# A three-block model on one core: products of constants on TensorE under the norms and turns, the head statistic of the gated linear attention in all partitions, the attention's modulation pair loaded beside its keys, the result stored in two halves

## What is computed

```python
x   = first_block(...)          # gated recurrence and gMLP in parallel, then a swiglu feed-forward, rmsnorm
mod = silu(c) @ mod_w[l] + mod_b[l]                       # 6 vectors for each layer l = 0, 1
h   = rmsnorm(x) * g * (1 + sc1) + sh1                    # "norm" below
y   = gla_mixer(h)         # layer 0: per head o = rmsnorm(o) over its 256 columns, times silu(og), @ w_out
y   = swa_sink_attention(h, w_q, sinks, w_out, k, v)      # layer 1: 16 heads, window of 128 keys
x   = x + g1 * y
h   = rmsnorm(x) * g' * (1 + sc2) + sh2
x   = x + g2 * peer(h)     # 16384 experts: hidden = gelu(h @ u.T), weighted by routes, @ v
k, v = shared_kv(rmsnorm(x) ...)                          # after layer 0
return rmsnorm(x) * g_final                               # 256 x 1024
```

## Time and profile before

| | |
|---|---|
| median of 3 runs | 2563.48 us (2561.51 to 2564.61) |
| the profiled execution's own time | 2558.92 us |
| its span, first to last instruction | 2557.1 us |
| busy: TensorE, VectorE, ScalarE, GpSimd | 97%, 71%, 49%, 3% of the span |
| mean granted TensorE clock | 0.984 of full speed |
| chain of waits that ended last | TensorE 86%, VectorE 6%, ScalarE 1%, DMA 1% |
| moved by DMA | 471.69 MB, 184 GB/s over the span |

### The profile page before, as it was taken

One profiled execution on the slowest core, in us unless ns is written; L12 is line 12 of the kernel. 1 busy time (PEld: TensorE's weight loads), 2 busy tenths in 40 slices (PEclk: granted clock), 3 DMA queues, 4 the chain that ended last, 5 costly groups with the idle time before them and its releaser, 6 DMA issues.

```text
span 2557.1 us, 43191 instructions
## 1 busy us (share of the span) xinstructions
PE 2470.6 (97%) x15988; PEld 2229.0 (87%) x15988; DVE 1808.5 (71%) x3476; ACT 1262.4 (49%) x2457; POOL 79.2 (3%) x42
## 2 busy tenths in 40 slices
PE   7999999999999999999999998889999999999997
PEld 4489889988899999999888887789999999888886
DVE  5566569863279967786888874759977787755554
ACT  2344134442234567775555453434557776445454
POOL 0000000000140000000000000041000000000000
PEclk9999999999999999999999999999999999999998
DMA  6553557645325543435888863143554344755552
GB/s 267 194 182 135 181 199 279 247 167 198 113 103 179 178 174 133 149 133 193 291 289 287 288 244 137 66 182 132 177 187 140 141 140 148 253 188 193 196 195 100
DMA packets 79176, 471.69 MB, mean 184 GB/s; under 512 B 8833, under 2 KB 9089, under 8 KB 26161
## 3 DMA queue, kind: packets, MB, share of 16 engines
q1 hardware_dynamic: 78480, 467.85, 51.4%
q10 hardware_dynamic: 272, 1.05, 0.1%
q0 software_dynamic: 272, 0.69, 0.1%
HBM read 468.51 MB, written 1.05 MB: 184 GB/s over the span
## 4 chain that ended last, share of the span: by engine, by line
PE 86%; DVE 6%; ACT 1%; DMA 1%; issue 1%; DVEq 0%; SPq 0%; ACTq 0%
PE bank L757 27%; PE bank L682 27%; PE bank L538 5%; PE bank L918 5%; PE bank L694 4%; PE bank L709 3%; PE bank L825 3%; PE bank L949 2%; PE bank L1013 1%; PE bank L548 1%; PE bank L1058 1%; PE bank L522 1%; DVE t_split L2002 1%; DVE macc L1744 1%; PE bank L554 1%
## 5 line engine op out<-in xcount | busy, mean ns | idle before, releaser
L682 PE MATMUL bank<-h_split,t_split 128*128 128x256 f32 x6144 | 772.3, 285 | 5.2 <-DVE t_split L2002 4.5
L682 PEld LDWEIGHTS bank<-h_split,t_split 128*128 128x128 f32 x6144 | 745.6, 192 | 7.5 <-DVE t_split L2002 5.9
L2002 DVE TENSOR_TENSOR t_split<-ring,t_split 128x1024 fp32r<-128x1024 f32 x512 | 624.9, 1221 | 159.5 <-ACT t_split L1236 158.0
L757 PE MATMUL bank<-t_split,w_split 128*128 128x512 f32 x3072 | 697.8, 390 | 1.1 <-ACT w_split L1243 1.1
L757 PEld LDWEIGHTS bank<-t_split,w_split 128*128 128x128 f32 x3072 | 576.5, 188 | 120.9 <-ACT w_split L1243 1.5
L1241 ACT ACTIVATE t_split<-ring 128x1024 fp32r<-128x1024 f32 x256 | 271.9, 1062 | 347.7 <-PE bank L757 219.4
L1236 ACT ACTIVATE t_split<-ring 128x1024 fp32r<-128x1024 f32 x256 | 271.0, 1059 | 295.1 <-PE bank L682 269.7
L2034 DVE TENSOR_TENSOR w_split<-arena,w_split 128x256 fp32r<-128x256 f32 x256 | 108.8, 425 | 194.0 <-ACT w_split L1243 193.6
L1163 ACT ACTIVATE arena<-bank 128x256 f32<-128x256 f32 (+2 forms) x160 | 63.8, 404 | 301.3 <-PE bank L709 68.1
L918 PE MATMUL bank<-h_split,wd_split 128*128 128x256 f32 x1056 | 129.2, 286 | 4.0 <-ACT h_split L1495 4.0
L918 PEld LDWEIGHTS bank<-h_split,wd_split 128*128 128x128 f32 x1056 | 128.1, 192 | 5.3 <-issue 4.3
(11 more groups left out here) (320 smaller groups left out, 2866.9 us busy)
## 6 DMA issues: line engine op xcount, KB each, us to landing
ring<-in_peer_u SPq DMA_DIRECT2D x128, 1024.0 KB, 4.9
ring<-in_peer_v SPq DMA_DIRECT2D x128, 1024.0 KB, 4.9
ring<-in_w_mod SPq DMA_DIRECT2D x24, 1024.0 KB, 5.0
ring<-in_mod_w SPq DMA_DIRECT2D x24, 1024.0 KB, 5.0
H<-in_mod_w SPq DMA_DIRECT2D x96, 256.0 KB, 5.2
ring<-in_w_in SPq DMA_DIRECT2D x22, 1024.0 KB, 5.7
ring<-in_w_up SPq DMA_DIRECT2D x22, 1024.0 KB, 4.9
ring<-in_peer_wq SPq DMA_DIRECT2D x16, 1024.0 KB, 5.0
```

The source lines that it names most:

```text
L682: last = mm(bank[:, 0:T], u[:, a_, k, :], h_split[:, b_, k, :], start=(k == 0 and a_ + b_ == 0), stop=(k == KT - 1 and a_ == 1))
L757: last = mm(BK[2 * tt + hf][:, :], w_split[:, j, a_, tt * P:(tt + 1) * P], t_split[:, 1 - j, b_, hf * 512:(hf + 1) * 512], start=(first an ...
L2002: TT(t_split[:, 1 - j, 1, :].rearrange("p (k c) -> p k c", k=KT), ring[:, r, :].rearrange(view, k=KT, j=2)[:, j], t_split[:, 1 - j, 0, :]. ...
```

## The change

- `turn_over(times)` is new on TensorE: it waits until the bank that the next tile will take is free, and multiplies `ones` by 512 columns of the constants into it, `times` times. Nobody reads the result; the next tile overwrites it. It stands behind the first modulation (2 products), behind the norms before the feed-forward, the GLA, both peers and the keys (4 each), in both rows_out ahead of the transposes (2 each), and behind the last norm (5): 31 products.
- ScalarE's wait for "x_free" moves from n = 0 to n = 1.
- The GLA head statistic is summed by products with all of `ones`, so it stands in all partitions at once; the scaling, root and reciprocal then run on 1024 columns in place of 8, and the diagonal and `lin_spread` fall away. The four `og` tiles stand together behind it.
- Layer 1's first modulation pair is loaded behind the two key panels and computed behind the first three ropes; the second stays in `swa_out`.
- The last norm raises "h" by 4 twice; the turns go by halves of the columns, and each half is stored on its own.

```diff
@@ -278,5 +278,5 @@
                     + peer_sections(0)
-                    + [(a["kv_k"], 2, "proj", 2), (a["kv_v"], 1, "proj", 2),
+                    + [(a["kv_k"], 2, "proj", 2), (a["mod_w1"], 2, "mod_acc", 1), (a["kv_v"], 1, "proj", 2),
                        (a["swa_q"], 4, "proj", 2)]
-                    + [(a["swa_out"], 1, "proj", 2), (a["mod_w1"], 2, "mod_acc", 1)] * 2 + [(a["swa_out"], 2, "proj", 2)]
+                    + [(a["swa_out"], 1, "proj", 2), (a["mod_w1"], 2, "mod_acc", 1), (a["swa_out"], 3, "proj", 2)]
                     + peer_sections(1))
@@ -434,3 +434,3 @@
 
-            sync.wait_ge(sems["out_done"], 16)
+            sync.wait_ge(sems["out_done"], 32)
 
@@ -515,2 +515,10 @@
 
+            def turn_over(times):
+
+                name = f"bank{4 + e.tile % 2}"
+                if e.fills.get(name):
+                    pe.wait_ge(sems[name], e.value(name, e.fills[name]))
+                for _ in range(times):
+                    mm(BK[4 + e.tile % 2][:, :], ones, con[:, 0:512], start=True, stop=True)
+
             def norm(src):
@@ -624,2 +632,8 @@
                 pe.wait_ge(sems["o_bank1"], e.more("o_bank1", 2))
+                if E == 2:
+                    for h in range(HEADS):
+                        for x in range(2):
+                            last = mm(BK[h // 2][:, h % 2 * T:(h % 2 + 1) * T], ones, osq[:, 2 * h + x, :], start=(x == 0), stop=(x == 1))
+                    last.then_inc(sems["oms"], 1)
+                    return
                 for h in range(HEADS):
@@ -640,2 +654,3 @@
 
+                turn_over(2)
                 pe.wait_ge(sems["y_out"], e.more("y_out"))
@@ -646,2 +661,3 @@
                 norm(hP)
+                turn_over(4)
                 pe.wait_ge(sems["sub_in"], e.more("sub_in", 16))
@@ -1038,5 +1057,3 @@
             lin_squares(M3, 2)
-            og_tiles(2)
-            lin_spread(M3["zA"])
-            og_tiles(2)
+            og_tiles(4)
             o8 = kt(M3["oT"], 8)
@@ -1071,2 +1089,3 @@
                     rot(m - 1, 2 if m == 1 else 3)
+            mod_between(2)
             w = next_panel().rearrange("p (k c) -> p k c", k=KT)
@@ -1131,3 +1150,3 @@
                 proj_cols(1, lambda k: oS[:, k, :], T)
-                if n < 2:
+                if n == 0:
                     mod_between(2)
@@ -1137,6 +1156,7 @@
             norm(hT)
+            turn_over(5)
 
-            pe.wait_ge(sems["h"], e.more("h", KT))
-            for tt in range(2):
-                for x in range(2):
+            for x in range(2):
+                pe.wait_ge(sems["h"], e.more("h", KT // 2))
+                for tt in range(2):
                     bank = ring_bank()
@@ -1436,3 +1456,3 @@
                 x_tiles(1)
-                if n == 0:
+                if n == 1:
                     act.wait_ge(sems["x_free"], 1)
@@ -1591,3 +1611,3 @@
             og_tiles(1)
-            lin_root(M3["dec"][:, 16:24])
+            lin_root(M3["zA"])
             og_tiles(4)
@@ -1655,8 +1675,11 @@
             y = H[:, :, :].rearrange("p k t -> p (k t)")[:, 0:2048].rearrange("p (a d) -> p a d", a=2)
-            for tt in range(2):
-                for x in range(2):
-                    evac("turn", y[:, tt, x * 512:(x + 1) * 512], ACT.Copy, width=512)
-            act.wait_ge(*e.tile_out())
-            act.dma_start(out.rearrange("o (a p) d -> p (o a) d", p=P), y).then_inc(sems["out_done"], 16)
-            act.wait_ge(sems["out_done"], 16)
+            rows = out.rearrange("o (a p) d -> p (o a) d", p=P)
+            for x in range(2):
+                part = slice(x * 512, (x + 1) * 512)
+                for tt in range(2):
+                    evac("turn", y[:, tt, part], ACT.Copy, width=512)
+                act.wait_ge(*e.tile_out(2))
+                act.wait_ge(*e.tile_out())
+                act.dma_start(rows[:, :, part], y[:, :, part]).then_inc(sems["out_done"], 16)
+            act.wait_ge(sems["out_done"], 32)
 
@@ -1795,4 +1818,4 @@
                         ins.then_inc(sems["hs"], 1)
-                if not shift:
-                    ins.then_inc(sems["h"], KT)
+                    elif k % 4 == 3:
+                        ins.then_inc(sems["h"], 4)
 
@@ -1887,4 +1910,9 @@
                     gate_block(b)
-                roots(M3["dec"][:, 16:24], root_buf, dv)
-                dve.wait_ge(sems["orep"], e.more("orep"))
+                dve.wait_ge(sems["oms"], e.more("oms"))
+                for pair in range(2):
+                    ins = TS(root_buf[:, pair * 512:(pair + 1) * 512], BK[pair][:, :], 1.0 / dv, EPS, MUL, ADD)
+                ins.then_inc(sems["ovar"], 1)
+                dve.wait_ge(sems["ostd"], e.more("ostd"))
+                dve.reciprocal(root_buf, root_buf).then_inc(sems["dve_step"], 1)
+                dve.wait_ge(sems["dve_step"], e.stepped())
                 for b in range(8):
@@ -1892,3 +1920,3 @@
                         dve.wait_ge(sems["dve_step"], gate_block(b))
-                    TT(oT[:, b, :], oT[:, b, :], BK[b // 4][:, b // 2 % 2 * T:(b // 2 % 2 + 1) * T], MUL).then_inc(sems["o_done"], 1)
+                    TT(oT[:, b, :], oT[:, b, :], root_buf[:, b // 2 * T:(b // 2 + 1) * T], MUL).then_inc(sems["o_done"], 1)
 
@@ -2464,3 +2492,3 @@
             norm(xT, hT, gain[:, 0, :], True)
-            used(3)
+            used(2)
 
@@ -2507,2 +2535,3 @@
                 rope(n)
+                mod_between(2, 16, 3 * n, min(3 * n + 3, KT))
             e.tiles("proj", 1)
@@ -2555,12 +2584,5 @@
                     e.tiles("turn", 2)
-            used(4)
-
-            def mods_behind(k):
-
-                if k % 2 == 0:
-                    used(1)
-                mod_between(2, 16, k % 2 * 4, k % 2 * 4 + 4)
-
-            residual("proj", 16, {k: lambda k=k: mods_behind(k) for k in range(4)})
-            used(2)
+            used(6)
+            residual("proj", 16, {k: lambda k=k: mod_between(2, 16, k * 4, k * 4 + 4) for k in range(2)})
+            used(3)
             mod_out((modc[:, 32:40], 0, V("mod_b_2")[:, 80:88]))
```

## The result

The changed kernel took 2532.45 us (median of 4 runs, 2523.96 to 2539.16), the kernel before 2563.65 beside it (4 runs, 2561.51 to 2564.61): a ratio of 0.9878, with a 95% interval of 0.9846 to 0.9909. That is faster by 31.2 us, where 32.1 were forecast. The execution that was profiled is the fastest of the four: 2523.96 us, span 2522.1.

The account below looks back on a forecast made before the run. TensorE, busy 97% of the span, bounds the kernel; its waits and half-clock time can be had. Terms 8.1 + 1.6 + 1.9 + 5.2 + 5.2 + 6.4 + 3.7 = 32.1 us give 2531.4 us (median), range 2525 to 2545.

Parts of the forecast that it names:

- Products under five norms: Four products fit in each norm's wait and the stretch behind starts at full clock: 8.1 us, bounds 0 and 17.
- behind the first modulation: Two products in a wait of 2.3 us there, so following products run at full clock: 1.6 us, bounds 0 and 1.7.
- in rows_out: Two products ahead of each rows_out's transposes, hidden in a 2.0 us wait: 1.9 us, middle of 0 to 3.7.
- the clock's share of the tail: Part of the last norm's gain that comes from full clock: about 1.5 us.
- Rival 2: Transposes lose the clock, products behind start at half; rows_out gives nothing: 27.7 us gained, 2535.8 us, chance 0.25.
- The statistic: GLA head statistic: 2.1 us fewer products plus 3.1 of half clock gone, 5.2 us, bounds 2 and 5.5.
- The cover of 3 us: At the GLA statistic, four og tiles (13.9 us) hide some 11 us of VectorE and ScalarE work, by 3 us.
- "x_free": Mixer's start: TensorE's 3.6 us wait goes, plus 1.6 for half clock behind: 5.2 us, bounds 2 and 5.5.
- The pair: Beside the keys: the projection's 4.34 us panel wait and half clock behind go, no cost: 6.4 us, bounds 4 and 6.5.
- The last norm and the store: At the end, earlier turns and store issue save 2.5, the half store 1.2: 3.7 us, bounds 1.2 and 4.2.
- Rival 1: The clock falls despite the products; 13.1 of 32.1 us goes, 19.0 left, 2544.5 us, chance 0.12.
- Rivals 3 and 4: 3: the change's panels collide, 2537.8 us, chance 0.05. 4: added products run at half clock, 2567.5 us, chance 0.02.

Follow-up runs that it names:

- the second one of the changed kernel: Profile from the second repeat of the changed kernel, nothing altered, run in the last batch; measured 2531.38 us, ratio 0.9887 to the kernel before.

## Why the prediction was right

*Products under five norms (8.1), behind the first modulation (1.6), in rows_out (1.9), and the clock's share of the tail (1.5): 13.1 in sum, measured 11.9.* The mechanism is as forecast: the products fit in the waits, the wait's end does not move, and the stretch behind runs at full clock, but not every time. By place the first profiles show 1.8 behind the feed-forward norm, 1.7 behind the GLA norm, 1.8 at the first peer's query. The 1.5 us for the second peer was 0.3 in the first profile and 1.9 in the second. What the forecast had wrong is that each stretch would come up for certain: behind the norms 14 of 60 stayed at half clock. With the first modulation it is 3.3 by place (113.7 against 110.4), more than the 1.6, since without the products the clock is at one half for 6.8 us there.

*rows_out: the middle of 0 and 3.7.* The doubt was whether transposes hold the clock. They do: the last norm's eight products behind them took 3.62 us. By place the way from the last value rows to the first key tile is 1.0 us shorter with the products than without, and the end 2.2, of which part is the last norm's own five. Rival 2 (0.25) is out, by the experiment with transposes most plainly.

*The statistic, 5.2.* 5.2 by place between the first profiles, 3.8 by the undone kernel, both by place and by the times: with the old statistic the clock was at half for 6.8 us in the one and for 3.4 in the other. The cover of 3 us was 3.2.

*"x_free", 5.2.* 5.6 by place and 3.0 by the times. The step that was mis-sized is the 1.6 us for the stretch behind: the clock does not stay up, it falls 50 us later at a wait that was there before. I had asked what is late next, and not where the clock falls next.

*The pair, 6.4.* 6.6 by the times. The price of the move was nothing, as forecast: no panel was late.

*The last norm and the store, 3.7, of which 2.2 without the clock.* 2.5 by place, 3.3 by the times; a half lands in 2.8 us, as taken.

The four undone parts add up to 16.7 us by the times, where 19.0 were forecast (the 3.7 of the tail without its 1.5 for the clock). Undone together, leaving the products alone, they cost 22.1; but by place the four are 17.9 of the 27.2 us between that profile and the second one of the changed kernel ("x_free" 3.7, statistic 5.2, pair 5.9, tail 3.1), and most of the rest is the late panel (3.3) and the half clock behind three norms (4.8). So the parts add up, with no sign that they need each other. The agreement of the whole, 31.2 against 32.1, is closer than that of the parts, and closer than the spread of the runs: in that it is luck. Rival 1 would have left 19.0, 2544.5 us; the kernel without products took 2543.42, which measures that world and shows it is not this one. Rivals 3 and 4 have no trace: no panel of the pair was late, and no block of added products at a norm took longer than at full clock. Behind the first modulation two blocks did, with the products alone (2.51 us in place of 1.96) and with transposes.

## What to carry to other kernels

Where TensorE bounded this kernel and waited for 2 to 4 us in front of dense work, the wait cost twice: once itself, once in the stretch at half clock behind. Work without a purpose, no longer than the wait, mostly took the second part away; it must end before the wait does (eight products in place of four: 6.2 us lost), and it should not stand ahead of an instruction for which the releaser of the next wait is waiting itself (the last heads' turns: nothing gained). Before the clock behind a removed wait is counted as gained, look for the next wait of like length: the fall of the clock may just move there, as from 157 to 207 us here.

## What the hardware showed that I had not expected

- fp32 transposes kept TensorE's granted clock up as well as products did: 2530.92 us against 2531.5.
- The same kernel has the clock at half behind a norm in one execution and not in the next. The changed kernel spreads over 15 us in the first comparison, and its times go with the mean granted clock of the run (0.998 to 0.993).
- In some executions, of several kernels, a panel of the first peer's stream comes late near 1215 to 1290 us, and TensorE waits up to 3.5 us in sum (2.99 in the one shown); in others, of the same stream at the same rate (205 GB/s over 720 to 1520 us, 204 in the one shown), there is no such wait. Why is open; no run tried it.
